# Norm and first projection of a two-layer transformer step in blocks of 512 columns of scale and shift

## What is computed

```
mod = silu_c @ w_ada + b_ada                      # (1, 6 * 2048)
shift_m, scale_m, gate_m, shift_f, scale_f, gate_f = split(mod, 6)
h = rmsnorm(x, g_norm_mix) * (1 + scale_m) + shift_m
proj = h @ w_in                                   # w_in: 2048 x 3904
dq, dk, dv, q_lat, kv_lat, k_pe = split(proj)     # 1024, 1024, 1024, 512, 256, 64 columns
dq, dk = partial_rope(dq), partial_rope(dk)
```

## Time and profile before

| what | us |
|---|---|
| median of 3 runs (lowest, highest) | 2817.53 (2814.77, 2822.38) |
| the profiled execution, its own time | 2800.4 |
| its span in the trace | 2798.7 |
| PE busy | 2655.8 (95%) |
| DVE, ACT, POOL busy | 1934.2, 1117.5, 172.1 |

### The profile page before, as it was taken

How to read it: one execution, slowest core, us unless ns; L and a number is a source line. 1 busy time by engine, 2 the same in 40 slices (tenths; PEclk the granted TensorE clock), 3 DMA queues, 4 the chain that set the end, 5 groups by cost and what they waited for, 6 DMA issues and landing times.

```text
span 2798.7 us, 54063 instructions
## 1 busy us (share of the span) xinstructions
PE 2655.8 (95%) x21548; PEld 2488.3 (89%) x21548; DVE 1934.2 (69%) x2015; ACT 1117.5 (40%) x1269; POOL 172.1 (6%) x281
## 2 busy tenths in 40 slices
PE   5799998899999999998998999999979999999998
PEld 1487787799999999997998989999959999999997
DVE  1345686787787776777867888888667566575664
ACT  2234443444443443334333444444433444344443
POOL 5000000101000010110000000000000000000000
PEclk8799999899999999999999999999979999999998
DMA  9887766578888887785766765567837666676763
GB/s 371 337 300 264 235 204 204 193 271 304 283 291 293 275 303 238 270 292 161 249 209 193 224 207 160 156 206 263 280 119 239 202 218 225 202 240 197 223 204 113
DMA packets 299843, 658.78 MB, mean 235 GB/s; under 512 B 30688, under 2 KB 37176, under 8 KB 295224
## 3 DMA queue, kind: packets, MB, share of 16 engines
q1 hardware_dynamic: 267448, 539.35, 57.9%
q0 software_dynamic: 32256, 117.45, 13.0%
HBM read 654.62 MB, written 2.10 MB: 235 GB/s over the span
## 4 chain that ended last, share of the span: by engine, by line
PE 86%; DVE 6%; DMA 4%; ACT 2%; issue 1%; SPq 0%; POOLq 0%; ACTq 0%; DVEq 0%
PE ps L1671 25%; PE ps L1672 25%; PE ps L1673 25%; DMA proj<-in_w_ada 2%; PE ps L1716 2%; PE ps L1718 2%; PE ps L1717 2%; DVE lo L943 1%; DMA ada_ring<-in_w_ada 1%; PE ps L1850 1%; ACT hi L566 1%; DMA raw<-in_w_in 1%; DVE work L955 1%; PE ps L2092 1%; PE ps L2113 0%
## 5 line engine op out<-in xcount | busy, mean ns | idle before, releaser
L943 DVE TENSOR_TENSOR lo<-raw,hi 128x1024 fp32r<-128x1024 f32 x868 | 1049.2, 1222 | 646.0 <-ACT hi L566 643.5
L566 ACT ACTIVATE hi<-raw 128x1024 fp32r<-128x1024 f32 x868 | 911.1, 1059 | 1310.7 <-PE ps L1673 1044.6
L1671 PE MATMUL ps<-acts,hi 128*128 128x256 f32 x4432 | 1253.1, 283 | 32.1 <-DVE lo L943 17.2
L1672 PE MATMUL ps<-acts,hi 128*128 128x256 f32 x4432 | 1239.2, 280 | 0.0
L1673 PE MATMUL ps<-acts,lo 128*128 128x256 f32 x4432 | 1238.9, 280 | 0.0
L1671 PEld LDWEIGHTS ps<-acts,hi 128*128 128x128 f32 x4432 | 841.6, 190 | 67.7 <-issue 41.6
L1673 PEld LDWEIGHTS ps<-acts,lo 128*128 128x128 f32 x4432 | 843.7, 190 | 0.4
L1672 PEld LDWEIGHTS ps<-acts,hi 128*128 128x128 f32 x4432 | 840.4, 190 | 2.2 <-issue 1.2
L1671 PE MATMUL ps<-f_acts,hi 128*128 128x256 f32 x2048 | 567.9, 277 | 4.9 <-DVE lo L943 4.9
L1672 PE MATMUL ps<-f_acts,hi 128*128 128x256 f32 x2048 | 566.6, 277 | 0.0
L1673 PE MATMUL ps<-f_acts,lo 128*128 128x256 f32 x2048 | 566.6, 277 | 0.0
(11 more groups left out here) (246 smaller groups left out, 1350.9 us busy)
## 6 DMA issues: line engine op xcount, KB each, us to landing
raw<-in_w_ff SPq DMA_DIRECT2D x512, 512.0 KB, 4.7
raw<-in_w_in SPq DMA_DIRECT2D x232, 512.0 KB, 4.7
ada_ring<-in_w_ada POOLq DMA_DIRECT2D x224, 512.0 KB, 4.9
proj<-in_w_ada SPq DMA_DIRECT2D x32, 1024.0 KB, 8.1
ada_ring<-in_w_ada SPq DMA_DIRECT2D x44, 512.0 KB, 4.7
work<-in_w_ada SPq DMA_DIRECT2D x32, 512.0 KB, 4.6
raw<-in_w_out SPq DMA_DIRECT2D x32, 512.0 KB, 5.2
raw<-in_w_o SPq DMA_DIRECT2D x32, 512.0 KB, 5.2
```

What stands on the lines that cost most here:

```text
L566: nc.scalar.activation(hi[n % SPLIT][:, :], raw[n % RAW][:, :], ACT.Copy).then_inc(hi_ready, 1)
L943: V.tensor_tensor(lo[n % SPLIT][:, :], raw[n % RAW][:, :], hi[n % SPLIT][:, :].bitcast(F32), ALU.subtract)\
L1671: M(out, h, right[:, 0:S], start=start, stop=False)
L1672: M(out, h, right[:, S:2 * S], start=False, stop=False)
```

## The change

Tiles of `w_ada` change their shape: 4 row tiles by 512 columns (still 1 MB, rows of 2 KB). Eight of them hold all rows of 512 columns of the scale (4 tiles) and of the shift (4 tiles), one *block* of four. After each four, ACT copies the row (`copy_block`), PE turns it with 4 one-column products (`turn_block`), DVE adds the bias (`finish_block`). Then the four tiles of h of the block are made (`block_normed`, `block_hi`, `block_low`).

The first three groups of `qk1` are open together, in banks 0 to 5. The two chunks of rows that belong to a block are taken for all three groups: 6 chunks per block (`PER_BLOCK`), 24 in all (`FIRST`), instead of 8 chunks of one group after the other. On PE a start tile of the next block stands behind each of the chunks 2 to 5 of a block, and the other four, with the two turns, between the blocks. In SP's queue the first two tiles of the next block stand ahead of chunks 4 and 5, the other six behind chunk 5, and then the next block's chunks. The root of the norm on ACT moves ahead of the sine table. The bank of the `w_ada` rows changes between 6 and 7.

Group 3 runs as before, over chunks 24 to 31. The turns of groups 0, 1 and 2 stand after its chunks 1, 3 and 5 on PE, the ropes after steps 2, 4 and 6 on DVE. The 32 pairs, in three buffers now, stand after chunks 24 to 62, four in every five chunks; two of them are issued ahead of chunk 24. The row of segment 2 is therefore turned one group later. Every count of `mod_ready`, `seg_reduced` and `rows_copied` falls by two.

```diff
+OPEN = 3
+BLOCKS = 4
+PAIRS, EARLY = 3, 2
...
+        FIRST = OPEN * FULL
+        PER_BLOCK = FIRST // BLOCKS
+        block_chunks = [(c, g) for c in range(FULL // BLOCKS) for g in range(OPEN)]
+        pair_after = {FIRST + 5 * p // 4: p for p in range(2 * KT)}
...
-            def start_tile(u, n, seg, row):
-                if n is not None:
-                    sp.wait_ge(ada_used, n)
-                sp.dma_start(start_ring[u], w_ada[0][row, seg * D:(seg + 1) * D]).then_inc(start_landed[u], 16)
-            for u in range(START):
-                start_tile(u, None, 0, slice(u * P, (u + 1) * P))
-            for s in range(2):
-                with sp.Fori(0, KT // START - (s == 0)) as i:
-                    for u in range(START):
-                        k = START * (s == 0) + u
-                        start_tile(u, i * (START * ADA) + ADA * (KT * s + k - START + 1), s, bass.ds(i * (START * P) + k * P, P))
+            def start_tile(n):
+                b, s, m = n // 8, 1 - n % 8 // 4, n % 4
+                if n >= START:
+                    sp.wait_ge(ada_used, ADA * (n - START + 1))
+                rows = w_ada[0][4 * P * m:4 * P * (m + 1), s * D + b * NC:s * D + (b + 1) * NC]
+                sp.dma_start(start_ring[n % START].rearrange("p (t n) -> p t n", n=NC), rows.rearrange("(t p) n -> p t n", p=P))\
+                    .then_inc(start_landed[n % START], 16)
...
-                if n % 2 and 0 <= (n - 3) // 2 < 2 * KT:
-                    ada_pair((n - 3) // 2)
+                if n - 1 in pair_after and pair_after[n - 1] >= EARLY:
+                    ada_pair(pair_after[n - 1])
             def ada_pair(p):
-                if p >= 2:
-                    sp.wait_ge(ada_used, ADA * (2 * KT + p - 1))
+                if p >= PAIRS - 1:
+                    sp.wait_ge(ada_used, ADA * (2 * KT + p - PAIRS + 1))
...
-            for pair in range(2):
-                groups(2 * FULL * pair, 0, w, 2 * pair * NC, FULL)
+            for b in range(BLOCKS):
+                for n in range(8 * b + (2 if b else 0), 8 * b + 8):
+                    start_tile(n)
+                for j, (c, g) in enumerate(block_chunks):
+                    n, k = PER_BLOCK * b + j, 4 * b + CK * c
+                    if j >= RAW and b + 1 < BLOCKS:
+                        start_tile(8 * (b + 1) + j - RAW)
+                    chunk(n, 0, (slot(n), w[:, k:k + CK, g * NC:(g + 1) * NC]))
+            for p in range(EARLY):
+                ada_pair(p)
+            for c in range(FULL):
+                n = FIRST + c
+                chunk(n, 0, (slot(n), w[:, CK * c:CK * c + CK, OPEN * NC:(OPEN + 1) * NC]))
...
+            def copy_block(i):
+                act.wait_ge(ada_used, ADA * START * (i + 1))
+                if i >= 2:
+                    act.wait_ge(turned_block, i - 1)
+                nc.scalar.activation(block_rows[i % 2], ps[:, 6 + i % 2, :], ACT.Copy).then_inc(rows_block, 1)
...
+            for b in range(BLOCKS):
+                copy_block(2 * b)
+                copy_block(2 * b + 1)
+                for j in range(2):
+                    split_chunk(PER_BLOCK * b + j)
+                act.wait_ge(mods_block, 2 * b + 2)
+                for c in range(FULL // BLOCKS):
+                    block_hi(b, c)
+                for j in range(2, PER_BLOCK):
+                    split_chunk(PER_BLOCK * b + j)
+            for j in range(SPLIT):
+                split_chunk(FIRST + j)
             act.wait_ge(angle_ready, 1)
             nc.scalar.activation(tables[:, :, :], tables[:, :, :], ACT.Sin).then_inc(sin_ready, 1)
-            norm_root()
-            def copy_rows(seg):
-                act.wait_ge(ada_used, ADA * KT * (seg + 1))
-                if seg:
-                    act.wait_ge(seg_reduced, seg)
-                nc.scalar.activation(mod_rows, ps[:, min(5 + seg, 6), :], ACT.Copy).then_inc(rows_copied, 1)
-            copy_rows(0)
-            for n in range(SPLIT):
-                split_chunk(n)
-            copy_rows(1)
-            act.wait_ge(mod_ready, 2)
-            norm_split("mix", shift=0)
-            for g in range(4):
-                group(FULL * g, g)
+            group(FIRST, OPEN)
...
-            finish_row(0)
-            for n in range(SPLIT):
-                split_chunk(n)
-            finish_row(1)
-            dve.wait_ge(mod_ready, 2)
-            norm_split("mix", xT, scale_cols(0, "g_norm_mix", 1), lambda t: mod(0, t), rstd)
...
+            for b in range(BLOCKS):
+                n0 = PER_BLOCK * b
+                finish_block(2 * b)
+                at = slice(4 * b, 4 * b + 4)
+                link(V.scalar_tensor_tensor(cols[:, 0, at], mods[:, KT + 4 * b:KT + 4 * b + 4], 1.0,
+                                            vecs[:, VEC["g_norm_mix"] + 4 * b:VEC["g_norm_mix"] + 4 * b + 4], ALU.add, ALU.mult))
+                for c in range(FULL // BLOCKS):
+                    block_normed(b, c)
+                finish_block(2 * b + 1)
+                split_chunk(n0)
+                block_low(b, 0)
+                split_chunk(n0 + 1)
+                block_low(b, 1)
+                for j in range(2, PER_BLOCK):
+                    split_chunk(n0 + j)
+            split_chunk(FIRST)
+            for g in range(OPEN):
+                split_chunk(FIRST + g + 1)
+                dve.wait_ge(weights_used, FIRST - OPEN + g + 1)
+                plain(proj[:, DQ + 4 * g:DQ + 4 * g + 4, :])(ps[:, 2 * g:2 * g + 2, :].rearrange("p b (j n) -> p (b j) n", n=S))
             dve.wait_ge(sin_ready, 1)
-            for g in range(4):
-                group(FULL * g, g, out=plain(proj[:, DQ + 4 * g:DQ + 4 * g + 4, :]),
-                      middle=g and (lambda: rope(proj[:, DQ + 4 * g - 4:DQ + 4 * g, :], cos_d, sin_d)) or None)
+            group(FIRST, OPEN, out=plain(proj[:, DQ + 4 * OPEN:DQ + 4 * OPEN + 4, :]),
+                  after={2 * g + 2: lambda g=g: rope(proj[:, DQ + 4 * g:DQ + 4 * g + 4, :], cos_d, sin_d) for g in range(OPEN)})
...
+            def start_tile(n):
+                i, m = n // START, n % START
+                pe.wait_ge(start_landed[m], 16 * (i + 1))
+                if m == 0 and i >= 2:
+                    pe.wait_ge(mods_block, i - 1)
+                for j in range(4):
+                    last = M(ps[32 * j:32 * j + 32, 6 + i % 2, :], silu_wide[:, 4 * m + j, :], start_ring[m][:, j * NC:(j + 1) * NC],
+                             start=m == 0, stop=m == START - 1)
+                last.then_inc(ada_used, ADA)
+            def turn_block(i):
+                pe.wait_ge(rows_block, i + 1)
+                for c in range(4):
+                    last = M(ps[:, 6 + i % 2, c:c + 1], block_rows[i % 2][:, c * P:(c + 1) * P], const("pick")[:, 0:1],
+                             start=c == 0, stop=c == 3)
+                last.then_inc(turned_block, 1)
...
+            for m in range(START):
+                start_tile(m)
+            spread_sum("mix")
+            turn_block(0)
+            for m in range(START):
+                start_tile(START + m)
+            turn_block(1)
+            for b in range(BLOCKS):
+                for j in range(PER_BLOCK):
+                    start_chunk(PER_BLOCK * b + j)
+                    if j >= 2 and b + 1 < BLOCKS:
+                        start_tile(8 * (b + 1) + j - 2)
+                if b + 1 < BLOCKS:
+                    start_tile(8 * (b + 1) + 4)
+                    turn_block(2 * b + 2)
+                    for m in range(5, 8):
+                        start_tile(8 * (b + 1) + m)
+                    turn_block(2 * b + 3)
...
-            for g in range(4):
-                group(FULL * g, g, pairs=True, fresh=normed_pieces("mix") if g == 0 else None,
-                      middle=g and (lambda: turn("turn_diff", proj[:, DQ + 4 * g - 4:DQ + 4 * g, :], g - 1)) or None)
+            group(FIRST, OPEN, pairs=True,
+                  after={2 * g + 1: lambda g=g: turn("turn_diff", proj[:, DQ + 4 * g:DQ + 4 * g + 4, :], OPEN - 1) for g in range(OPEN)})
```

More of the change, by code:

```diff
@@ L198, in build @@
         norm_tmp, kv_norm_tmp = proj[:, 32:48, :], proj[:, 30:32, :]
+        block_tmp = [proj[:, 48 + 4 * i:52 + 4 * i, :] for i in range(2)]
         sq_sum, sq_piece = proj[:, 48:52, :], [proj[:, 52:56, :], cross]
@@ L328, in pieces_of @@
             tiles = norm_tiles[name]
+            if name == "mix":
+                return [(t, t + 2) for t in range(0, KT, 2)]
             return [(0, 2), (2, 4), (4, 8), (8, 12), (12, 16)] if tiles == KT else [(0, tiles)]
@@ L734, in _ @@
             n0, g0 = first["v1"]
-            group(n0, g0, after=diff_step(0, {0: lambda: copy_rows(2)}))
-            group(n0 + FULL, g0 + 1, after=diff_step(1))
+            group(n0, g0, after=diff_step(0))
+            group(n0 + FULL, g0 + 1, after=diff_step(1, {3: lambda: copy_rows(2)}))
             group(*first["qlat"], after=diff_step(2))
@@ new lines, in block_normed, with block_low @@
+            def block_normed(b, c):
```

(39 more changed lines are left out.)

94 lines of the change are left out of this document (48 added, 46 removed).

## The result

The changed kernel is **slower**: 2836.5 us median of 20 runs against 2817.4 of 20 runs of the kernel before, ratio 1.0074 with a 95% interval of 1.0047 to 1.0101. The quotient of the two medians is 1.0068; the ratio is taken over the fast runs alone. The forecast was 2816 with a range from 2800 to 2832, so the time came out above the range, and the change costs time where I had it win 1.5 us. The profiled executions differ by 2815.6 - 2798.7 = 16.9 us of span.

A forecast was written before the change was run, and what follows sets the result against it. It took the start to be bound by DMA and the projection after it by PE. A gain of 6.9 us by chunk 24 and 5.4 lost to ropes gave -1.5 us: 2816 us, range 2800 to 2832.

The forecast's parts named there:

- What bounds: Start of the kernel: bound by DMA from 23 to 100 us; the projection after it bound by PE.
- the border at chunk 24: Where old and new chunk order meet again: chunk 24 starts at 170.8 against 177.7, 6.9 us gained.
- My way: Last wait before chunk 24: PSUM banks are free 3.6 us after chunk 22's end, so it waits 0.9 us.
- block 0: First block of the start: its first chunk begins at 44.9 us.
- intervals: Block to block in the start: 32.7 us plus clock, 3.0 for block 0 and 2.5 for the others.
- travel of the last tile: Boundary between blocks: the last start tile's DMA takes 5.6 us, with 5.3 and 6.6 kept as alternatives.
- The estimate of 4.7: Last tile's travel from some 2.0 us fixed cost per transfer: 4.7 us, making three boundaries 2.7 us cheaper.
- the clock: Block boundaries: PE falls to half clock at each, costing 3.0 us for block 0 and 2.5 for the others.
- The ropes: Group 3, chunks 24 to 31: PE waits 2.1 and 3.3 us for ropes on DVE, 5.4 us lost, bounds 0 and 8.
- "Later": Chunks 24 to 62: denser pairs, third buffer and renumbered waits cost nothing; late pairs would cost 1 to 2 us each.
- Rival (d): Denser pairs come late, or rope delay runs into attention of group `v1`: +6 to +15 us, 2822 to 2831; chance 0.04.
- The sum: Whole kernel: 6.9 us gained at the start and 5.4 lost to the ropes, -1.5 us in all.

The follow-up runs named there:

- one chunk: Changed kernel with every pair DMA from pair 2 on one chunk later in SP's queue; ratio 0.9987 to the kernel before the change.
- The old kernel with the short lead: Kernel before the change with each pair DMA one odd chunk (two chunks) sooner in SP's queue; ratio 1.0073 to the unaltered kernel before.
- two chunks: Changed kernel with every pair DMA from pair 2 on two chunks later in SP's queue; ratio 0.9998 to the kernel before the change.
- the ropes alone: Changed kernel with the three ropes on DVE one step sooner, after steps 1, 3 and 5 of group 3; ratio 1.0038 to the kernel before.

## Why the prediction was wrong, step by step

**What bounds, and the border at chunk 24: right.** Forecast 170.8, measured 171.55. The chain of the trace comes to chunk 24 by another way than mine: a raw chunk that travelled 10.0 us from 155.72, behind the two early pairs, then ACT, DVE and the copies. My way ends at the same time, so nothing was lost by it: PE had used chunk 22 at 167.8, and 3.6 more are 171.4. Single terms: block 0 at 47.0 against 44.9 (the last tile and its turn ran at half clock, 1.94 and 1.87 us, and lay on the chain); intervals 35.0, 34.8 and 34.6 against 35.7 and 35.2; travel of the last tile 5.1 against 5.6. The estimate of 4.7 for it in the prediction rests on a fixed cost that the Trainium skill (DMA: Bandwidth & Descriptors, Anatomy of one DMA) gives for transfers that POOL issues; these are SP's, and 5.1 is what counts. The first three chunks of a block took 11.5, 11.1 and 10.6 instead of 8.2 us, so the clock cost 3.3, 2.9 and 2.4 against 3.0 and 2.5. In block 3 PE's steps are 0.21 us until 155.5 and 0.12 after it, so four us at half cost 2.0 there. The Trainium skill (TensorE: Matmul & The Clock Gate, HAM oscillation) has a PE that waits for DMA put back to the lower clock each time. The trace agrees as far as every block paid, each behind a wait of 2.7 to 3.3 us, though the last to end was a wait for DVE's low part. It is not so behind every wait: behind the second rope wait of 3.3 us the clock was at half in the changed kernel (turn 2.46 us) and at full with one chunk (1.98).

**The ropes: right as waits.** Forecast 2.1 and 3.3 us, measured (timeline of PE, changed kernel):

```profile
190.11 1.98 PE L1829 MATMUL ps<-proj,consts_sb 128*128 128x512 f32 x4 [2.06 <-DVE proj L1178]
...
202.02 2.46 PE L1829 MATMUL ps<-proj,consts_sb 128*128 128x512 f32 x4 [3.28 <-DVE proj L1178]
```

Taking them out gave 6.2 to 9.4 us counted from chunk 24, least where the clock had stayed at full. So the waits were sized right (5.3 against 5.4), and the clock behind them, and what stood behind, which I had called nothing, were left out.

**"Later" is the step that failed.** I priced the denser pairs at nothing, because "a pair's three buffers let it be issued nearly four chunks (some 14 us) ahead". That lead is the pair's own. What counted was the lead of the chunk queued behind the pair on SP: I never wrote down who waits behind SP's wait. It went from 7 chunks to 5 or 6. ACT may split a chunk once PE has used the chunk four before it. By the unit costs of the prediction, an estimate, a chunk that leaves 5 ahead has one chunk and at most one pair of PE's time until then, 2.7 to 3.9 us; 6 ahead it has 5.5 to 7.9, and 7 ahead 8.2 or more. The travel was 5.7 us. PE alone need not feel a split that is a few us late, since `lo` is made up to four chunks ahead; but ACT and DVE take their attention and rope steps in program order behind that split, and PE waits for these. The old kernel with the short lead shows the same: 2.0 us lost over the first four groups, 18.7 among the attention steps. Rival (d) named the place, with the other cause (late pairs), 0.04 of chance and a price of 6 to 15. Order alone gave back 19.3 us (two chunks) and 23.3 (one), 17.8 and 20.9 counted from chunk 24. The bound behind "nothing" was 1 to 2 us per pair, over 32 pairs; the range did not take it in.

**The sum.** With the lead put back by one chunk, the latents' copy is at 355.14 against 356.01 before: -0.9 us where I had -1.5. The sum comes out for a kernel with that one line changed, in part by luck: chunk 24 began 1.6 us sooner there than I had it (169.2 against 170.8), and from there to the copy it took 186.0 us, where 160.5 before, 17.8 of moved work and 5.4 of ropes make 183.7, that is 2.3 more. Shown by runs: the queue (order alone cures it, order alone brings it to the old kernel). Seen in one trace each, and not separated by a run: that the difference between one and two chunks is clock, and that part of the ropes' extra gain is.

## What to carry to other kernels

A load queue that waits for a buffer holds up everything queued behind it: before moving such a wait, count for the *next* item how far ahead of its consumer it now leaves, and compare with travel time plus the in-order work of every engine between, not with the slack of the last one. Where transfers are interleaved, put the one with the tight buffer behind the ones that others need soon; here one position moved the ratio from 1.0074 to 0.9987. When work is spread over a stretch that was bound by DMA, count all of PE's work into the new interval, that at its border too (30 of 35 us here, not 21).

## What the runs showed of the hardware

The feed-forward loops, the same code in all kernels, have two paces. PE is busy throughout at a granted clock of 1.00, but in 200 us it does 1767 matmuls in one execution and 1701 in another, 200 / 1767 = 0.113 and 0.118 us each. The windows of the kernel before, and of the kernel with pairs two chunks later:

```profile
700.00:900.00 200.00, 200.00 (x1767) 200.00 (x1766) 151.67 (x128) 81.56 (x78) 19.25 (x37) 1.00 0.87 289
```

```profile
700.00:900.00 200.00, 200.00 (x1701) 200.00 (x1700) 146.07 (x123) 78.02 (x75) 18.81 (x36) 1.00 0.84 279
```

In the second, the stretch from 546 to 1303 us is some 20 us longer than in the kernel before (544.7 to 1282.1), with the same 6218 matmuls in it. In the kernel with the ropes alone it was the last feed-forward instead (3398 matmuls in 400 us against 3529), and its span is 2837.6 beside a median of 2814. So the pace can differ within one execution: that kernel's first feed-forward was at the quick pace, and the last one of the kernel with pairs two chunks later as well (3532). The runs of this latter kernel lie in heaps: five from 2790 to 2800, five from 2819 to 2824, one at 2850. One feed-forward at the slower pace, some 20 us, would make about such a distance; that the heaps come from it is not shown, for there is one trace of each kernel. The heaps make the intervals wide, so that 5 us at the start can't be read from medians. What sets the pace stays open; no run here separates it.
